# Attention in a two-block transformer kernel: scaling by the row sums inside the transposition, with a scaled identity matrix

## The reference

```python
_, sel = lax.top_k(iscore, topk)             # 128 keys for each query, by an indexer
s = jnp.einsum("bqngd,bqknd->bngqk", qg, ksel) * scale
p = jax.nn.softmax(s, axis=-1)
o = jnp.einsum("bngqk,bqknd->bqngd", p, vsel)
# 8 query heads of 128, 2 key/value heads; keys of later chunks are not admitted
```

## Time and profile before

| | us |
|---|---|
| median of the three runs | 3881.51 |
| lowest and highest | 3881.3, 3883.84 |
| profiled execution, its own time | 3880.74 |
| its span from first to last instruction | 3878.9 |
| TensorE matmul busy | 3581.2 (92%) |
| VectorE busy | 2435.0 (63%) |
| GpSimd busy | 2064.2 (53%) |
| ScalarE busy | 1010.7 (26%) |
| granted TensorE clock, mean | 0.959 |

### The profile page before, as it was taken

How to read it: one execution, slowest core, us unless ns; L and a number is a source line. 1 busy time by engine, 2 the same in 40 slices (tenths; PEclk the granted TensorE clock), 3 DMA queues, 4 the chain that set the end, 5 groups by cost and what they waited for, 6 DMA issues and landing times.

```text
span 3878.9 us, 49891 instructions
## 1 busy us (share of the span) xinstructions
PE 3581.2 (92%) x20100; PEld 3064.2 (79%) x20100; DVE 2435.0 (63%) x2980; ACT 1010.7 (26%) x1772; POOL 2064.2 (53%) x1100
## 2 busy tenths in 40 slices
PE   7999788899999999978889999999988878899997
PEld 7898678899999879856777788777867764588886
DVE  6686788777832658678987873485234554563335
ACT  4306432122110330643222110111014333322201
POOL 4355235465666535422546776676644442366664
PEclk9899899999999989989999999999989988999999
DMA  3122011222323312211222342343224332222232
GB/s 131 50 92 73 32 40 60 71 82 94 126 90 100 104 50 93 66 33 44 65 71 92 131 145 98 101 142 122 98 104 162 111 114 73 74 92 92 99 107 71
DMA packets 96899, 348.31 MB, mean 90 GB/s; under 512 B 10848, under 2 KB 13152, under 8 KB 93664
## 3 DMA queue, kind: packets, MB, share of 16 engines
q1 hardware_dynamic: 80064, 289.44, 22.4%
q10 hardware_dynamic: 16672, 56.70, 3.8%
HBM read 322.32 MB, written 23.79 MB: 89 GB/s over the span
## 4 chain that ended last, share of the span: by engine, by line
PE 66%; DVE 22%; ACT 8%; issue 3%; POOL 0%; DMA 0%; ACTq 0%; DVEq 0%; POOLq 0%
PE acc L473 19%; PE acc L474 19%; PE acc L476 19%; DVE cu L1890 7%; PE aux L624 1%; DVE rh L1846 1%; DVE ptmp L2051 1%; PE aux L694 1%; PE aux L774 1%; PE aux L709 1%; ACT us L1455 1%; DVE rb L1843 1%; PE acc L723 1%; ACT yv L1490 1%; DVE mtmp L1725 1%
## 5 line engine op out<-in xcount | busy, mean ns | idle before, releaser
L446 POOL TENSOR_SCALAR whi<-raw 128x1024 fp32r<-128x1024 f32 x548 | 638.1, 1164 | 1740.9 <-PE acc L476 1719.6
L448 POOL TENSOR_TENSOR wlo<-raw,whi 128x1024 fp32r<-128x1024 f32 x548 | 1426.3, 2603 | 45.7
L473 PE MATMUL acc<-nhi,whi 128*128 128x512 f32 (+1 forms) x2776 | 957.3, 353 | 55.3 <-DVE mt L1899 24.3
L474 PE MATMUL acc<-nlo,whi 128*128 128x512 f32 (+1 forms) x2776 | 949.6, 351 | 0.0
L476 PE MATMUL acc<-nhi,wlo 128*128 128x512 f32 (+1 forms) x2776 | 870.5, 349 | 0.0
L473 PEld LDWEIGHTS acc<-nhi,whi 128*128 128x128 f32 x2776 | 528.1, 190 | 142.4 <-issue 56.2
L473 PE MATMUL acc<-bhi,whi 128*128 128x264 f32 (+1 forms) x1864 | 560.5, 317 | 24.6 <-ACT rg L1141 11.8
L474 PEld LDWEIGHTS acc<-nlo,whi 128*128 128x128 f32 x2776 | 527.5, 190 | 67.8
L474 PE MATMUL acc<-blo,whi 128*128 128x264 f32 (+1 forms) x1864 | 546.4, 309 | 0.0
L476 PEld LDWEIGHTS acc<-nhi,wlo 128*128 128x128 f32 x2776 | 488.9, 190 | 68.5
L1890 DVE SCALAR_TENSOR_TENSOR cu<-cx,par,cu 128x528 f32<-128x528 f32 (+1 forms) x480 | 484.0, 1062 | 0.0
(11 more groups left out here) (351 smaller groups left out, 4567.3 us busy)
## 6 DMA issues: line engine op xcount, KB each, us to landing
raw<-in_w SPq DMA_DIRECT2D x548, 512.0 KB, 3.3
kept_cp<-pcp ACTq DMA_DIRECT2D x4, 1280.0 KB, 6.7
cp<-kept_cp ACTq DMA_DIRECT2D x4, 1280.0 KB, 11.1
kept_ap<-pap ACTq DMA_DIRECT2D x4, 1024.0 KB, 4.0
kept_cs<-pcs ACTq DMA_DIRECT2D x4, 1024.0 KB, 6.4
ap__140<-kept_ap ACTq DMA_DIRECT2D x4, 1024.0 KB, 5.5
cs__150<-kept_cs ACTq DMA_DIRECT2D x4, 1024.0 KB, 6.6
merge_gates<-gout ACTq DMA_DIRECT2D x16, 256.0 KB, 3.0
```

The costliest lines, as they stand in the source:

```text
L446: pool.tensor_scalar(hi, w, 1.0, 0.0, ALU.mult, ALU.add).then_inc(sem("w_hi"), 1)
L448: pool.tensor_tensor(lo, w, hi.bitcast(F32), ALU.subtract).then_inc(sem("w_split"), 1)
L473: pe.matmul(acc[s][:, f, 0:TH], hi, xh[:, f * TH:(f + 1) * TH], start=a, stop=False)
L474: pe.matmul(acc[s][:, f, 0:TH], hi, xl[:, f * TH:(f + 1) * TH], start=False, stop=False)
```

## The change

ScalarE no longer scales the tile of exponentials. It scales the 128x128 identity matrix by the reciprocals instead, row by row, into a tile `rdiag` of its own, and TensorE multiplies the exponentials' pieces (as the stationary operand) by this diagonal matrix. The outcome is the same: the transposed piece, each of its columns scaled. The instruction is a plain fp32 matmul where a transposition stood. `rdiag` lies at the address of `mt`, which is used in the next stage. Both layers of the first block are changed; the second block's attention is not.

```diff
         sg, o = at("sg", [P, T1], o)
+        rdiag, _ = at("rdiag", [P, P], o)
         mt, o = at("mt", [P, T1], o)
...
                     for c, w in pieces(W):
-                        m = pe.transpose(aux[1][0:w, c // 4, (c % 4) * P:(c % 4) * P + r], sm[0:r, j % 3, c * P:c * P + w],
-                                         ident[0:r, 0:r])
+                        m = pe.matmul(aux[1][0:w, c // 4, (c % 4) * P:(c % 4) * P + r], sm[0:r, j % 3, c * P:c * P + w],
+                                      rdiag[0:r, 0:r], start=True, stop=True)
                     m.then_inc(sem("at_turned"), 1)
...
                 def share(j):
                     b = j % 3
-                    r, W = (P, META + (items[j][1] + 1) * P) if items[j][1] < NQT else (META, META)
+                    r = P if items[j][1] < NQT else META
                     act.wait_ge(sem("at_share"), n0 + j + 1)
-                    act.activation(sm[0:r, b, 0:W], sm[0:r, b, 0:W], ACT.Copy, scale=rrs[0:r, b:b + 1]).then_inc(sem("at_p"), 1)
+                    act.activation(rdiag[0:r, 0:r], ident[0:r, 0:r], ACT.Copy, scale=rrs[0:r, b:b + 1]).then_inc(sem("at_p"), 1)
```

## The result

The changed kernel takes 3890.28 us (median of 12 runs, 3887.35 to 3897.58), the kernel before 3882.6 (12 runs, 3880.08 to 3883.99): a ratio of 1.0023, 95% interval 1.0014 to 1.0032. So it is slower by 7.7 us, or 0.23%: little, but the interval leaves 1 out. Forecast was 3878.5, 3.0 less than the kernel before, between 3869 and 3890. The profiled execution of the changed kernel took 3892.59 us, its span is 3890.8, 11.9 more than before.

A forecast was written before the change was run, and what follows sets the result against it. No engine fills the attention stretches; a ring of TensorE, ScalarE and VectorE bounds them. 7.8 + 3.7 - 15.7 + 1.3 for one fall left = -2.9 us: 3877.8 profiled, 3878.5 as median, range 3869 to 3890.

The forecast's parts named there:

- +11.5 for the pieces: Both attention stages: net path cost of dearer pieces and shorter share, 7.8 us in layer 0 plus 3.7 in layer 1.
- -14.4 for the clock: Both stages: low-clock stretches vanish and give back 15.7 us, less 1.3 for one left in place.
- step 1: TensorE: each of 232 pieces takes two records instead of one, 0.11 us more a piece, 26 us of TensorE time.
- upper bound: TensorE: 0.14 us more a piece, from whole groups, (1.47 - 0.77) / 5; 33 us of TensorE time.
- step 3: Layer 0: what of the longer pieces and shorter share lies on the path, +0.86 us a head, +7.8 in all.
- cover: Layer 0's 5-piece item: GpSimd's split holds VectorE's tap anyway, absorbing the later start; +0.15 us instead of 0.54.
- Heads over 26.3 us: Layer 0 at full clock: heads of 26.3 us or more would show the delay is not absorbed; 25.9 was expected.
- step 4: Layer 1: +0.32, -0.34, +0.54, -0.12 us for items with 3, 4, 5, 2 pieces; +0.40 a head, +3.7 in all.
- step 2: ScalarE: scaled tile shrinks to 128 columns, 0.40 us; saves up to 0.34 an item, 11 us of ScalarE time.
- step 5: TensorE's clock: twelve falls cost 15.7 us; matmuls keep the clock up where transpositions do little, so one fall stays.
- The sentence on the Trainium skill's clock rule: TensorE: a transpose does not count as busy time for the clock as a matmul does, so all 15.7 us return.
- the cover is not there: Rival: VectorE's tap is not held and a piece costs 0.14; +6 us, 3888, milder form 3884; chance 0.15.

The follow-up runs named there:

- before_fill: The kernel before, with idle matmuls in TensorE's waits for ScalarE in both layers: 3867.56 us, ratio 0.9963.
- twice_fill: The kernel before with every transposition issued twice, without idle matmuls despite its label: 3889.6 us, ratio 1.002.
- wide_fill: The changed kernel with each item's last piece 128 columns wide and idle matmuls in TensorE's waits: 3881.41 us, ratio 0.9999.
- share_fill: The kernel before with ScalarE scaling an identity nobody reads, division by row sums left out, idle matmuls in TensorE's waits: 3858.91 us, ratio 0.9941.
- transpose_fill: The kernel before with idle fp32 transpositions of the identity in TensorE's waits, twice as many as the idle matmuls they replace: 3868.88 us, ratio 0.996.
- matmul_alone: The kernel before with TensorE's pieces as plain fp32 matmuls by the constant identity, ScalarE still scaling the whole tile: 3893.75 us, ratio 1.003.

## Why the prediction was wrong

The forecast was a difference of two terms of like size, +11.5 for the pieces and -14.4 for the clock. In the stages it came out as +22.3 and -11.5: the clock's term is the 15.8 us that the falls cost before (before_fill) less the 4.2 they still cost, and the other is what is then left of the +10.8.

- *The price of a piece (step 1) failed, and this decides.* The group of 10 records for V stood in the earlier trace rows with 1.47 us, and the upper bound drawn from it, 0.14 a piece, was set aside because "the upper value holds V's slow 16-row piece". The new product has a piece of that kind too, the last one with 16 columns. Groups came out at 0.37, 0.48, 0.60 and 0.71 us above the transpositions' instead of 0.21, 0.32, 0.43 and 0.54. For 5 pieces that is the whole difference of the two groups (0.70); for 2 pieces it is over 0.18 a piece, above the upper bound of 0.14, since the addition is there once for each group. A further 0.2 us lies behind the groups of 3 and 5 pieces. Transpositions with the same 16-column piece, from which the lower bound was drawn, do not have this step. Splitting the path price of a layer 0 head: second record +0.8, narrow piece +0.55, shorter share -0.2; the rest of the 1.4 us, +0.3, is left for other differences of matmul and transposition. Of layer 1: +0.85, +0.57, -0.47, rest +0.15, together 1.1 (from twice_fill, wide_fill, share_fill and the changed kernel). So the second record alone was priced rightly.
- *The path of layer 0 (step 3)* was right in its working but for 0.13 and 0.06 us too much at the item with 5 pieces and meta, as the doubled transpositions show; its cover was sized for 0.11. With the true price V ends late enough to pass GpSimd's hold: the item with 5 pieces grew by 0.46 and not by 0.15, that with 3 by 0.60 (forecast 0.32), that with 4 by 0.47 (0.43). Heads over 26.3 us were named as the sign that the cover fails; they came with the cover there, by the price.
- *Layer 1 (step 4)*: the item with 5 pieces grew by 0.9, forecast 0.54; that with 3 by 0.60, forecast 0.32; that with 4 and the shorter share by -0.26, forecast -0.34.
- *The share (step 2)* was right: 401 ns measured, 400 forecast, and 0.12 and 0.34 us saved where it is waited for.
- *What falls cost before (step 5)* was right: 15.7 forecast, 15.8 given back by filling, some 0.5 of it at the stages' starts.
- *That the change takes the falls away (step 5)* failed. Seven of twelve stayed, against one forecast. The reason given, that transpositions do little for the clock, is false here: twice_fill and transpose_fill. It had been read from two stretches, with busy times 1.76 and 1.93 us, too near each other to carry it. What came back, 11.5 us, came back because there are fewer falls, and because five of the seven now lie in an item where TensorE is hardly waited for and cost 0.06 to 0.4 us each instead of 1.5. Why fewer is not shown: more records alone leave six (twice_fill) or seven (matmul_alone), but the shorter share alone, with no record added, leaves eight. That they moved was not forecast and is luck: nothing in the change aims at it.
- *The sentence on the Trainium skill's clock rule*, that by it all 15.7 us come back, went with this. The other one, that a logical transposition should not be a plain matmul, would have given the sign.
- *The rivals*: "the cover is not there", at a piece price of 0.14, gave 3888 and was the nearest; its mechanism is the price and the cover passed, though the clock gave less back than it took for granted.

The stages differ by +10.8 us and the medians by +7.7. The profiled executions, from which the stages are read, differ by 11.9, so that only 1.1 us lies outside the stages; the rest is that the changed kernel's profiled execution is 2.3 us above its median and the kernel's before 1.9 below.

## What to carry to other kernels

When a bound comes from the very form that will be used, such as the group of products with the same narrow last piece, take its whole difference before explaining part of it away. When a forecast is the difference of two terms of like size, state the chance that the sign turns, not only the spread of each. And where TensorE's waits let its clock fall at items that others wait for, idle matmuls or transpositions in those waits can be worth more than shortening the work itself: 14 us here, 21 with those at the stages' starts, against 5 us that the shorter share gives at full clock. Where the waits are short and the falls cheap they give nothing, as in the changed kernel.

## What the runs showed of the hardware

- A plain fp32 matmul whose stationary operand is 16 columns wide, between products with 128 columns, costs about 0.1 us ahead of it and 0.2 us behind it: 1.66 against 1.37 us from the group with 5 pieces to the weight products. If the next product is 16 columns wide too, nothing is lost at this place (1.23 us in both). fp32 transpositions of the same shape show no such step (0.77 us for five).
- Transpositions hold TensorE's granted clock at 1.00 in place of matmuls: no fall in both stages with transpositions in the gaps, behind the low clock at their starts. The Trainium skill, TensorE: Matmul & The Clock Gate, PE-mode transpose, has it otherwise: it does not count them as busy time in the same way. For fp32 here the measurement decides.
- Twelve stretches of 3.4 us at the low clock cost some 15.5 us, 1.3 each, but between nothing and 1.7 by the item in which they lie.
- Where the clock falls repeated from one execution to another, nearly to the item: 18 of 19 falls in two executions of each of the two kernels.
